# One decoder layer with a top-4-of-32 MoE on one core: router logits computed expert-major in four column groups, slot numbers counted from one

## What is computed

```python
h2 = rmsnorm(x1, g_ffn) * (1 + sc2) + sh2          # sc2, sh2 differ for prompt and samples
logits = x @ w_router + b_router                   # (264, 32)
top_v, top_e = lax.top_k(logits, TOP_K)            # 4 of 32 experts
gates = softmax(top_v)
...                                                # tokens sorted by expert, one block after another
gu = xb @ w_gu[e] + b_gu[e]                        # (rows, 2048), 8 MB of weights an expert
glu = min(gate, 7) * sigmoid(1.702 * min(gate, 7))
y = ((clip(up, -7, 7) + 1) * glu) @ w_d[e] + b_d[e]   # 4 MB of weights an expert
```

## Time and profile before

| | |
|---|---|
| median of three runs | 1308.48 us |
| lowest, highest | 1308.03, 1311.05 us |
| profiled execution, span from the first to the last instruction | 1316.4 us |
| PE busy | 1190.6 us (90%) |
| DVE busy | 322.6 us (25%) |
| ACT busy | 174.7 us (13%) |
| read from HBM | 496.48 MB, 380 GB/s over the span |
| chain that ended last | PE 70%, DMA 25%, ACT 2% |

### The profile page before, as it was taken

One profiled execution on the slowest core, in us unless ns is written; L12 is line 12 of the kernel. 1 busy time (PEld: TensorE's weight loads), 2 busy tenths in 40 slices (PEclk: granted clock), 3 DMA queues, 4 the chain that ended last, 5 costly groups with the idle time before them and its releaser, 6 DMA issues.

```text
span 1316.4 us, 15254 instructions
## 1 busy us (share of the span) xinstructions
PE 1190.6 (90%) x5966; PEld 606.0 (46%) x5966; DVE 322.6 (25%) x586; ACT 174.7 (13%) x344; POOL 48.4 (4%) x95
## 2 busy tenths in 40 slices
PE   5999999999999989897898979898988989897997
PEld 2788756788643424343242424243342424242433
DVE  2379865333222011102001110111020011101133
ACT  2132231100210200110020002001100200020012
POOL 0121231000000000000000000000000000000000
PEclk9999999899798999899999999999989999898998
DMA  9998999975679999999999999999999999999993
GB/s 353 352 348 306 375 331 399 358 287 188 228 321 416 409 415 420 415 403 418 417 419 415 422 414 422 414 421 416 418 418 417 420 414 422 414 421 409 418 415 120
DMA packets 106349, 500.50 MB, mean 380 GB/s; under 512 B 8761, under 2 KB 10919, under 8 KB 70848
## 3 DMA queue, kind: packets, MB, share of 16 engines
q1 hardware_dynamic: 99456, 478.38, 90.6%
q0 software_dynamic: 6576, 21.42, 4.5%
q10 hardware_dynamic: 272, 0.09, 0.0%
HBM read 496.48 MB, written 3.38 MB: 380 GB/s over the span
## 4 chain that ended last, share of the span: by engine, by line
PE 70%; DMA 25%; ACT 2%; issue 1%; DVE 1%; SPq 1%; DVEq 0%
PE ps L959 26%; DMA ring<-in_w_d 23%; PE ps L460 11%; PE ps L1027 11%; PE ps L1129 4%; PE ps L899 3%; PE ps L825 2%; PE ps L780 2%; DMA ring<-in_w_ada 2%; PE ps L394 2%; PE ps L849 1%; PE ps L425 1%; PE ps L634 1%; PE ps L915 1%; ACT oT L1406 1%
## 5 line engine op out<-in xcount | busy, mean ns | idle before, releaser
L959 PE MATMUL ps<-ring,zone 128*64 128x512 f32 x2000 | 442.8, 597 | 20.9 <-DMA ring<-in_w_gu 18.7
L1027 PE MATMUL ps<-ring,oT 128*64 128x512 f32 x1024 | 250.4, 646 | 63.9 <-DMA ring<-in_w_d 63.9
L959 PEld LDWEIGHTS ps<-ring,zone 128*64 128x64 f32 x2000 | 144.1, 138 | 315.8 <-issue 299.3
L1027 PEld LDWEIGHTS ps<-ring,oT 128*64 128x64 f32 x1024 | 88.2, 148 | 224.0 <-issue 224.0
L1970 DVE TENSOR_SCALAR zone<-ps 128x1024 f32<-128x1024 f32 x15 | 18.4, 1225 | 593.2 <-PE ps L959 593.2
L460 PE MATMUL ps<-hT,ring 128*128 128x264 f32 x640 | 150.3, 393 | 2.1 <-DVE hT L1557 1.8
L460 PEld LDWEIGHTS ps<-hT,ring 128*128 128x128 f32 x640 | 121.4, 192 | 29.6 <-issue 8.3
L1396 ACT ACTIVATE attn<-zone 128x1024 f32<-128x1024 f32 x15 | 15.8, 1057 | 459.0 <-DVE zone L1970 459.0
L1987 DVE TENSOR_TENSOR zone<-zone,ps 128x264 f32<-128x264 f32 x56 | 24.0, 429 | 147.5 <-PE ps L1129 147.5
L394 PE MATMUL ps<-ident,zone 128*128 128x128 f32 (+3 forms) x212 | 32.2, 277 | 15.8 <-DMA zone<-in_b_alpha 10.1
L899 PE MATMUL ps<-zone,tok 128*128 128x224 f32 x224 | 44.2, 356 | 0.1
(11 more groups left out here) (382 smaller groups left out, 798.3 us busy)
## 6 DMA issues: line engine op xcount, KB each, us to landing
ring<-in_w_gu SPq DMA_DIRECT2D x123, 2048.0 KB, 17.5
ring<-in_w_d SPq DMA_DIRECT2D x62, 2048.0 KB, 17.3
ring<-in_w_ada SPq DMA_DIRECT2D x12, 2048.0 KB, 11.0
ring<-in_w_in SPq DMA_DIRECT2D x9, 2048.0 KB, 12.3
ring<-in_cache_k SPq DMA_DIRECT2D x32, 256.0 KB, 7.3
ring<-in_cache_k POOLq DMA_DIRECT2D x32, 256.0 KB, 6.5
ring<-in_cache_v SPq DMA_DIRECT2D x32, 256.0 KB, 10.7
ring<-in_cache_v POOLq DMA_DIRECT2D x32, 256.0 KB, 8.6
```

The source lines that it names most:

```text
L959: ins = pe.matmul(ps[64 * j:64 * j + CAP, c, :], xg[:, k, 2 * par + j, :], rows, start=False, stop=(k == KT - 1), skip_group_check=True)
L1027: ins = pe.matmul(ps[64 * j:64 * j + CAP, 4 + c, :], hidT[:, k, j * CAP:(j + 1) * CAP], w[j][:, kk, c * 512:(c + 1) * 512], start=(k == 0) ...
```

## The change

- *Constant part* (behind m = 4 of stage 1): `w_r[:, k, :]` becomes the stationary operand (32 columns), the nine shift columns the moving one. Block k goes to column group k % 4 of the array, that is to PSUM partitions 32(k % 4) to 32(k % 4)+31, so each group holds a partial sum over two blocks. DVE copies the 9 columns to `shift_parts`. Behind m = 5 two matmuls with `row_in_32` (a 128x32 matrix with a one where the row is congruent to the column modulo 32) add the four parts and turn them.
- *Raw logits*: the experts are stationary (32 columns), the 256 prompt tokens or 8 samples move; block k goes to column group k % 4. They are issued in three pieces: blocks 0 to 3 behind m = 5 of the output products, blocks 4 to 6 behind the last one, block 7 after the first sums of squares. DVE copies all 264 columns to SBUF (`raw_parts`). Three products with `row_in_32` add the four parts and turn them token-major, ahead of stage 3. PE waits for that copy.
- *Banks*: sums of squares move from bank 5 to bank 7, cleared at another place by DVE; the turned logits and the places lie in bank 6; the counts in bank 4; the third and fourth piece of the turn go to banks 7 and 5, and PE waits for `x1_var` ahead of the third.
- *Choice*: `keys8[:, :, 4:8]` is set to 3e38 early, so that one copy (L1922) goes.
- *Places*: the order of the five products stays; DVE is told after the third. The largest count is taken after `pick`. `slots_iota` counts from 1, so that the subtraction of one (L1944) goes.
- Ten named semaphores become two counters, one for PE's steps and one for DVE's.

```diff
-H2_BANKS = (0, 1, 6, 7)
+H2_BANKS = (0, 1, 7, 5)
...
+ROUTE_PE = ("raw_full", "x1_sums", "raw_summed", "places", "counts")
+ROUTE_DVE = ("raw_taken", "x1_var", "x1_inv", "chosen", "top_shift")
...
                     for k in range(KT):
-                        pe.matmul(bank[:, 0:NE], modT[:, 24 + k, 0:1].to_broadcast([P, P]), w_r[:, k, :],
-                                  start=(k == 0), stop=(k == KT - 1))
-                    for k in range(KT):
-                        ins = pe.matmul(bank[0:NS, NE:2 * NE], modT[:, 24 + k, 1:9], w_r[:, k, :],
-                                        start=(k == 0), stop=(k == KT - 1))
-                    vector_filled(ins, "shift_logits")
+                        rows = slice(NE * (k % 4), NE * (k % 4) + NE)
+                        ins = pe.matmul(bank[rows, 0:9], w_r[:, k, :], modT[:, 24 + k, 0:9],
+                                        start=(k < 4), stop=(k >= 4), skip_group_check=True)
+                    vector_filled(ins, "shift_parts")
+                if m == 5:
+                    from_vector("shift_parts")
+                    bank = vector_bank()
+                    pe.matmul(bank[:, 0:NE], shift_parts[:, 0:1].to_broadcast([P, P]), row_in_32, start=True, stop=True)
+                    vector_filled(pe.matmul(bank[0:NS, NE:2 * NE], shift_parts[:, 1:9], row_in_32, start=True,
+                                            stop=True), "shift_logits")
...
-            def raw_logits(k):
-
-                pe.wait_ge(sig("x1"), k + 1)
-                for t in range(2):
-                    pe.matmul(ps[:, 5, t * NE:(t + 1) * NE], xT[:, k, t * P:(t + 1) * P], wr_gain[:, k, :],
-                              start=False, stop=(k == KT - 1), skip_group_check=True)
-                pe.wait_ge(sig("xs_gain"), k + 1)
-                pe.matmul(ps[0:NS, 5, 2 * NE:3 * NE], xs_gain[:, k, :], w_r[:, k, :],
-                          start=False, stop=(k == KT - 1), skip_group_check=True)
+            def raw_logits(numbers):
+
+                pe.wait_ge(sig("x1"), numbers[-1] + 1)
+                for k in numbers:
+                    rows = slice(NE * (k % 4), NE * (k % 4) + NE)
+                    pe.matmul(ps[rows, 5, 0:TP], wr_gain[:, k, :], xT[:, k, 0:TP],
+                              start=(k < 4), stop=(k >= 4), skip_group_check=True)
+                pe.wait_ge(sig("xs_gain"), numbers[-1] + 1)
+                for k in numbers:
+                    rows = slice(NE * (k % 4), NE * (k % 4) + NE)
+                    ins = pe.matmul(ps[rows, 5, TP:T], w_r[:, k, :], xs_gain[:, k, :],
+                                    start=False, stop=(k >= 4), skip_group_check=True)
+                return ins
...
-                if m >= 2:
-                    raw_logits(m - 2)
+                if m == 5:
+                    raw_logits(range(4))
             freed["wo0"] = freed["wo1"] = (vector_full, len(v_index))
-            raw_logits(KT - 2)
+            raw_logits(range(4, KT - 1))
             pe.wait_ge(sig("sq_sum"), 1)
             token_squares(sq_sum, False)
-            raw_logits(KT - 1)
+            raw_logits(range(KT - 1, KT)).then_inc(routed("raw_full")[0], 1)
             pe.wait_ge(sig("x1_sq"), KT)
-            token_squares(sq_zone[:, KT - 1, :], True).then_inc(sig("x1_sums"), 1)
+            token_squares(sq_zone[:, KT - 1, :], True).then_inc(routed("x1_sums")[0], 1)
+
+            pe.wait_ge(*routed("raw_taken"))
+            for t, (t0, tn) in enumerate(TOK_TILES):
+                ins = pe.matmul(ps[0:tn, 6, t * NE:(t + 1) * NE], raw_parts[:, t0:t0 + tn], row_in_32,
+                                start=True, stop=True)
+            ins.then_inc(routed("raw_summed")[0], 1)
...
-            pe.wait_ge(sig("chosen"), 1)
-            bank = ps[:, 5, 256:512]
+            pe.wait_ge(*routed("chosen"))
+            bank = ps[:, 6, 256:512]
             pe.matmul(bank[:, 0:NE], before[:, :], chosen[:, 0, :], start=True, stop=True)
             pe.matmul(bank[:, NE:2 * NE], ones[:, :], chosen[:, 0, :], start=True, stop=False)
-            pe.matmul(bank[:, NE:2 * NE], before[:, :], chosen[:, 1, :], start=False, stop=True)
...
+            pe.matmul(bank[:, NE:2 * NE], before[:, :], chosen[:, 1, :], start=False, stop=True)\
+                .then_inc(routed("places")[0], 1)
+            pe.matmul(ps[:, 4, 0:NE], ones[:, :], chosen[:, 0, :], start=True, stop=False)
+            pe.matmul(ps[:, 4, 0:NE], ones[:, :], chosen[:, 1, :], start=False, stop=True)\
+                .then_inc(routed("counts")[0], 1)
...
-            dve.wait_ge(sig("x1_sums"), 1)
+            dve.wait_ge(*routed("raw_full"))
+            V.tensor_copy(raw_parts, ps[:, 5, 0:T]).then_inc(routed("raw_taken")[0], 1)
+            dve.wait_ge(*routed("x1_sums"))
...
-            V.tensor_copy(keys8[:, :, 0:4], top8[:, :, 0:4])
-            chain(V.tensor_copy(keys8[:, :, 4:8], top8[:, :, 0:1].to_broadcast([P, 3, 4])))
+            chain(V.tensor_copy(keys8[:, :, 0:4], top8[:, :, 0:4]))
...
-            chain(V.tensor_reduce(rounds_f[:, 0:1], bank[:, 3 * NE:4 * NE], AX_X, ALU.max))
...
-            chain(V.tensor_scalar(place[:, 0:2, :], place[:, 0:2, :], -1.0, None, ALU.add))
...
+                dve.wait_ge(*routed("counts"))
+                chain(V.tensor_reduce(rounds_f[:, 0:1], ps[:, 4, 0:NE], AX_X, ALU.max))
```

More of the change, by code:

```diff
@@ L264, in decoder_step @@
         sq_sum = part(zone, ALLP, 2112, T)
+        raw_parts = part(attn_flat, ALLP, 352, T)
+        shift_parts = part(attn_flat, ALLP, 616, 9)
         x1_inv = tiny(P, 3 + NS)
@@ L284, in decoder_step, with routed @@
         named = {}
+        route_pe, route_dve = sem("route_pe"), sem("route_dve")
+        def routed(name):
+            steps = ROUTE_PE if name in ROUTE_PE else ROUTE_DVE
+            return route_pe if name in ROUTE_PE else route_dve, steps.index(name) + 1
         def sig(name):
@@ L840, in _ @@
                 t, g = n // 2, n % 2
+                if n == 2:
+                    pe.wait_ge(*routed("x1_var"))
                 for k in range(4):
@@ L1359, in _ @@
             squares("x1", "x1_sq")
-            act.wait_ge(sig("x1_var"), 1)
+            act.wait_ge(*routed("x1_var"))
             nc.scalar.activation(x1_inv, x1_inv, ACT.Sqrt).then_inc(sig("x1_rms"), 1)
-            act.wait_ge(sig("x1_inv"), 1)
+            act.wait_ge(*routed("x1_inv"))
             for n in range(4):
@@ L1905, in _ @@
                     .then_inc(sig("xs_gain"), 1)
-            dve.wait_ge(sig("x1_sums"), 1)
-            V.tensor_scalar(x1_inv, ps[:, 5, 96:99 + NS], 1.0 / D, EPS, ALU.mult, ALU.add).then_inc(sig("x1_var"), 1)
+            dve.wait_ge(*routed("raw_full"))
+            V.tensor_copy(raw_parts, ps[:, 5, 0:T]).then_inc(routed("raw_taken")[0], 1)
+            dve.wait_ge(*routed("x1_sums"))
+            V.tensor_scalar(x1_inv, ps[:, 7, 0:3 + NS], 1.0 / D, EPS, ALU.mult, ALU.add).then_inc(routed("x1_var")[0], 1)
             dve.wait_ge(sig("x1_rms"), 1)
-            V.reciprocal(x1_inv, x1_inv).then_inc(sig("x1_inv"), 1)
-            dve.wait_ge(sig("x1_inv"), 1)
+            V.reciprocal(x1_inv, x1_inv).then_inc(routed("x1_inv")[0], 1)
+            dve.wait_ge(*routed("x1_inv"))
+            dve.wait_ge(*routed("raw_summed"))
             for t in range(3):
-                ins = V.scalar_tensor_tensor(out=logits[:, t, :], in0=ps[:, 5, t * NE:(t + 1) * NE],
-                                             scalar=x1_inv[:, t:t + 1], in1=logit_bias[:, t, :],
+                rows = TOK_TILES[t][1]
+                ins = V.scalar_tensor_tensor(out=logits[0:rows, t, :], in0=ps[0:rows, 6, t * NE:(t + 1) * NE],
+                                             scalar=x1_inv[0:rows, t:t + 1], in1=logit_bias[0:rows, t, :],
                                              op0=ALU.mult, op1=ALU.add)
@@ L1926, in _ @@
             chain(ins)
-            V.tensor_tensor(chosen, rest, logits, ALU.not_equal).then_inc(sig("chosen"), 1)
+            V.tensor_tensor(chosen, rest, logits, ALU.not_equal).then_inc(routed("chosen")[0], 1)
             V.tensor_tensor(logits, logits, top8[:, :, 0:1].to_broadcast([P, 3, NE]), ALU.subtract)\
-                .then_inc(sig("top_shift"), 1)
+                .then_inc(routed("top_shift")[0], 1)
             chain(V.tensor_tensor(xs_gain, xs_gain, x1_inv[:, 3:3 + NS].unsqueeze(1).to_broadcast([P, KT, NS]),
@@ L2252, in load_expert @@
                         if i == 7:
-                            sp.wait_ge(sig("x1_sums"), 1)
+                            sp.wait_ge(*routed("x1_sums"))
                             load_whole_spare(7)
```

22 lines of the change are left out of this document (11 added, 11 removed).

## The result

The changed kernel takes 1301.25 us in the median of five runs (1299.66 to 1302.64). The kernel before, with two more runs, stays at 1308.48 (1307.78 to 1313.2). The ratio is 0.9934 with a 95% interval of 0.9913 to 0.9955: between 5.9 and 11.4 us faster. The forecast was 2.7 us and the range ended at 1302.7, so the time lies outside it, on the side that was forecast.

A forecast was written before the change was run, and what follows sets the result against it. The weight stream bounds the second half, and PE's position before it sets its start. Savings of 3.07 us less 0.40 give 2.7 us, taken from the 1308.5 us median: 1305.8 us, eight times in ten from 1302.7 to 1308.9.

The forecast's parts named there:

- What bounds the kernel: Whole kernel: the weight stream bounds the second half, and a microsecond PE saves ahead of 398 us moves everything behind it.
- Step "Constant part": Shift products: eight thin matmuls at 0.07 us, 0.08 a burst, 0.28 for the sum; 2.26 us becomes 0.92, saving 1.34.
- Step "Raw logits ahead of T": Until the last output product ends (T): five bursts, 2.55 us, become one of 0.82, saving 1.73 us.
- Step "Behind T": From the end of the last output product (T) to the turn: 4.67 us instead of 4.27, so 0.40 later.
- The added waits: PE's and DVE's new waits around the turn: all covered, the copy of `raw_parts` ending 0.8 us before PE needs it.
- Step "Turn, bias, places, gather": From the turn to the gather: no term on PE; choice and `pick` stay off the path, margins growing to 3.3 and 1.7 us.
- Step "the clock falls there again": Behind the last output product: clock falls to 1.2 GHz within the second squares as before; three new products take 1.01 us.
- Rival 1: Router's 17 us at the lower clock changes by 3.4 us: shorter gives 1304.1 us (chance 0.22), longer 1307.5 (0.10).
- Rival 4: Router: the choice is on the path after all, so places and counts save 1.2 us more, 1304.6 us; chance 0.04.

The follow-up runs named there:

- e6: The changed kernel with 6 useless matmuls of 264 moving columns between the sums and the turn: 1306.64 us, ratio to before 0.9961.
- e9: The changed kernel again, no edit, with a second trace: 1301.70 us, ratio to before 0.9941.
- e8: The changed kernel with all eight raw-logit blocks in one column group instead of four: 1304.41 us, ratio to before 0.9941.
- e4: The kernel before with only the new choice, places and slot numbers: 1308.17 us, ratio to before 0.9998.
- e5: The changed kernel with 13 useless matmuls of one moving column between the sums and the turn: 1310.66 us, ratio to before 0.9992.
- e12: The kernel before with 13 useless matmuls of one moving column ahead of its turn: 1314.75 us, ratio to before 1.0042.
- e7: The kernel before with 6 useless matmuls of 264 moving columns ahead of its turn: 1312.70 us, ratio to before 1.0017.
- e2: The kernel before with only the new raw logits in four column groups: 1305.91 us, ratio to before 0.9955.
- e10: The changed kernel with the choice, places and slot numbers of the kernel before: 1300.99 us, ratio to before 0.9929.
- e1: The kernel before again, no edit, with a second trace: 1310.12 us, ratio 1.0002.

## Why the prediction was wrong

**What bounds the kernel: right.** PE's position before the experts sets the weight stream's. Over the fourteen traces the experts' first product starts anywhere from 338.7 to 357.2 us, and what follows takes 960.0 to 964.7 us all the same. The stream's stretch did not shrink, and e6's 2.8 us of added work cost the changed kernel 2.6 us in the mean (4.9 us under its kernel before, e9 7.5).

**Step "Constant part": too dear.** Eight matmuls with 32 stationary and 9 moving columns take 0.24 us together, not 8 x 0.07 + 0.08: in four groups the thin ones overlap too (e8 shows it for the samples: four matmuls take 0.23 us in one group and 0.05 in four). The bound "all thin ones four abreast" was the right end. 1.72 us saved for 1.34.

**Step "Raw logits ahead of T": one term missing.** The burst takes 0.61 for my 0.82. And the output block behind each burst was slower: 3.76 us, against 3.60 in the changed kernel's run of six (21.63 / 6). I priced the burst, not the block after it. From the first to the end of the last output product 2.77 us are saved, for 1.73. Such an entry price is there behind the new burst as well: the two blocks behind it take 7.32 us, and at the 3.57 of a further block in the run of six (21.63 less 3.76, over 5) the first of them took 3.75. The Trainium skill (TensorEngine Tiling (Array Packing), "Key Properties") says that changing the tiling mode drains the engine. No run here shows that this is the price: the old burst, with 128 and 8 stationary columns, and the new one, with 32 in four groups, are followed by blocks of the same length, and a weight load that could not be pulled ahead would look alike. What the change saved is the number of such entries.

**Step "Behind T": 0.40 us for nothing.** At 2.4 GHz the work from T to the turn takes 3.83 us before (e4's chain, from 328.62 to 332.45) and 3.77 after: the turn is no later. I had made it 0.40 later, because I priced the three new products at the lower clock, at 1.01 us; they took 0.62. The added waits cost nothing, as written: the copy of `raw_parts` ended 0.5 us before PE asked for it.

**Step "Turn, bias, places, gather": one term missing.** I gave it nothing. At 2.4 GHz the old kernel's gather waits 0.6 us for `pick` and the new one's does not.

At full clock, work therefore gives 1.72 + 2.77 + 0.06 + 0.62 = 5.2 us and not 2.7. This alone, 1303.3, would have been inside the range. (The range's low end, 1302.7, was 0.6 below what its two terms, 1.7 and 0.8, make of 1305.8.)

**Step "the clock falls there again": the one that failed.** It kept the 17 us at 1.2 GHz for the changed kernel, and carried "2.7 us earlier at the gather" over to the median with it. They were 0 in the one trace of after and 3.4 in the other. When they came they cost 7.2 us of L. It also made the 0.40 above and hid the 0.6. Rival 1 had the right sign, at 1304.1, but I let the stretch shrink by one short fall of 3.4 us. How much of the result is the clock is known only as what the work leaves over: 7.2 less 5.2, 2 us, by the medians, and anything from 0.7 to 6.2 by the interval; the traces' 3.3 us fit in. That the content of this stretch moves the time by some 4 us at equal work was shown twice (e5 against e6, e12 against e7). Why the fall comes in some executions of the same kernel and not in others, and stays down for 3.4 us or for 17, is open.

**Rival 4 (the choice is on the path).** I called its cover 2.5 us and 0.4 us. Both were margins at half clock; at 2.4 GHz the first is nil (e4) and the second negative, minus 0.6 us (e2, e10). In time it made no difference that e4 or e10 could show.

**The trace that all this was read from.** Its span was 7.9 us over the median of the runs, more than the whole effect. I noted it and carried the sum over unscaled. The profiled and a timed execution differ by 1.75 us in the changed kernel (1299.5 and 1301.25, the same execution), so a span of 1316.4 meant an execution of some 1318 us, later than every one of the 99 recorded. The low stretch in the router was not what made it so: e1 has the same one in an execution of 1310.47 us. The excess lay in stretches that I had not looked at, 3.55 us ahead of the output products and 4.0 behind the experts' first. What the low stretch spoiled was the reading of the rows in it, and my own rows held the other case: the same gather in 3.75 us instead of 6.71.

## What to carry to other kernels

When a row lies in a stretch at the lower clock, work the sum out once with its duration there and once at full clock; here margins on other engines changed sign between the two, and a term was priced at 1.01 us that took 0.62. When a span lies well above the timed runs, compare it with a second trace of the same kernel, stretch by stretch, before you name the cause: here it was not the stretch that stood out. A stretch of narrow matmuls, transposes and sums can cost TensorE more than its own time, because the clock may stay down for what follows; in e5 against e6 the same 2.8 us in other matmuls was worth 4 us. Price a small burst by the block behind it as well.

## What had not been expected of the hardware

- The clock went to 1.2 GHz while PE was busy 4.00 of 4.00 us (e1). The Trainium skill (TensorE: Matmul & The Clock Gate, "Why this matters for your kernels") asks that idle gaps be avoided to prevent drops. Here there was no gap, and the same 2.8 us in matmuls of 1 moving column or of 264 moved the mean by 4 us.
- A matmul with 256 moving columns in each of three or four column groups costs 0.56 us in all, the same as one alone (0.55). In one group, four take 1.84 us and three 1.41, so four groups are 3.3 times as fast and three 2.5 times, entry included. The Trainium skill (TensorE: Matmul & The Clock Gate, "Measured speedup vs the span model") gives 2.38 for three column tiles with 512 moving columns; the measured 2.5 is a little above it.
- Untouched stretches differ between executions: the 960 us behind the experts' first product by up to 4.7 us (960.0 to 964.7), and in two traces of the same kernel the output products start at 295.22 and at 298.77.
